# The experts' width in two chunks of 1408 instead of 1024, 1024 and 768, smaller weight units in byte rings, and the sixteen experts written out

## The chip, the core and the metric

The kernel runs on one core of one Trainium2 chip. The metric is the device time in microseconds of one execution, given as the median of three runs. The names of the engines are those of the profile: PE is TensorE (matmuls and transposes), PEld its weight loads, DVE is VectorE, ACT is ScalarE, POOL is GpSimd and SP is SyncE, which here only issues DMAs.

## The reference

The reference is one layer of a hybrid diffusion block: a mixer (long convolutions and a state-space model) and then a mixture of 16 experts, in which each expert picks 128 of the 1024 latent tokens. Only the mixture is touched by the change:

```python
def expert_choice_ffn(h, router_w, w_gate, w_up, w_down):
    n, dm = h.shape[1], h.shape[2]
    cap = CAPACITY_FACTOR * n // N_EXPERTS
    aff = jax.nn.softmax(jnp.einsum('bnd,de->bne', h, router_w).astype(jnp.float32), axis=-1)
    gates, idx = lax.top_k(jnp.swapaxes(aff, 1, 2), cap)
    xg = jax.vmap(lambda hb, ib: hb[ib])(h, idx)
    def expert(args):
        xe, wg, wu, wd = args
        return (jax.nn.silu(xe @ wg) * (xe @ wu)) @ wd
    ...
```

For each expert xe is 128 x 1024, gate and up weights are 1024 x 2816, the down weight is 2816 x 1024, all in float32. That is 34.6 MB of weights for each expert and 554 MB for the sixteen; every weight is read once.

## The kernel before

The program has six stages: prepare, mix, long_convs, output_and_route, experts and finish. The stage experts takes most of the span, and the change lies in it, in the class Weights that lays out its weights, and in two numbers of output_and_route.

**Three products for one.** PE multiplies in the type fp32r, and to keep float32's precision each operand is split in a high part (ACT copies it to fp32r, L2117) and a low part (DVE subtracts the high part from the original, L2152, in place over the original). PE then multiplies high by high, low by high and high by low (L2085 to L2087 for gate and up, L2098 for down). So each weight passes from HBM by a DMA (L1963) to ACT, to DVE and to PE.

**Units.** The weights of an expert come in 18 units, which all engines count in the same order. The width of 2816 is cut into chunks of 1024, 1024 and 768. Each chunk has four units: gate and up, each in two halves of four contraction tiles (4 x 1024 or 4 x 768 elements in each partition). Units 12 to 17 are the down weights, five of four tiles and one of two. A unit has one of six slots of 16 KB for the original and the low part, and one of three slots of 16 KB for the high part.

**The order on each engine** is written out by hand and kept by semaphores. While PE multiplies unit n, ACT makes the high part of unit n + 2 and DVE the low part of unit n + 1. A high part may be written once PE has done with the unit three before it (`used`), and SP may issue a load once PE has done with the unit six before it. Between these stand the other steps of an expert:

- after the gate half of a chunk, ACT takes Silu from PSUM (L2134); after the up half DVE multiplies it by up (L2170); one unit later PE transposes the product (L2066), ACT and DVE make its high and low part (L2138, L2174). PE waits for this low part (`alo`) at the first down unit that uses it.
- the tokens of the next expert are gathered by POOL (L2037), transposed by PE after unit 15 (L2055), and split by ACT (L2121, `high_tokens`) and DVE (L2156, `low_tokens`) in the step of unit 16.
- at the end of an expert DVE scales the result in PSUM to SBUF (L2179) and POOL adds it to the output in HBM (L2043).

DVE's last steps for an expert e stand in this order:

```python
    elif not last_e:
        low_part(e + 1, 0)
...
dve.wait_ge(used, multiplied(e, UNITS - 1))
dve.wait_ge(idxr, 2 * e + 1)
nc.vector.scalar_tensor_tensor(ye, ps[:, 6:8, :]..., ALU.mult, ALU.mult).then_inc(yev, 1)
```

The first fifteen experts are one hardware loop on each engine (`experts_of`, Fori, L1998), the sixteenth is written out behind it.

Of the kernel before, what the change touches and what calls it, by code (L numbers as in the profile page):

```python
# [7 lines left out]
F32 = mybir.dt.float32  # L8
# [1675 lines left out]
def output_and_route(k):  # L1684
# [26 lines left out]
    with nc.Block() as block:  # L1711
        @block.sync
        def _(sp):
# [10 lines left out]
            for n in range(3):  # L1724
                k.weights.load(sp, 0, n)
# [3 lines left out]
            for n in range(3, k.weights.NS):  # L1729
                k.weights.load(sp, 0, n)  # L1730
# [198 lines left out]
class Weights:  # L1929
# [3 lines left out]
    chunks = [(0, 1024), (1024, 1024), (2048, FF - 2048)]  # L1933
    NCW = len(chunks)
    FT = FF // P
    KH = KD // 2
    NS, NHI = 6, 3
    DOWN = 4 * NCW
    tiles = [min(4, FF // P - 4 * d) for d in range(-(-FF // 512))]
    UNITS = DOWN + len(tiles)  # L1940

    def __init__(self, k):
        assert self.UNITS % self.NS == 0 and self.UNITS % self.NHI == 0
        self.raw = [k.over(f"w_raw{s}", 16 * s, 16, F32) for s in range(self.NS)]
        self.got = [k.ctx.enter_context(k.nc.semaphore(f"e_got{s}")) for s in range(self.NS)]
        self.gate_up = [k.i[n].rearrange("l e (k p) f -> l e p k f", p=P) for n in ("ex_w_gate", "ex_w_up")]
        self.down = [k.i["ex_w_down"][:, :, 512 * d:512 * d + P * t, :].rearrange("l e (p f) n -> l e p f n", p=P) for d, t in enumerate(self.tiles)]

    def elements(self, n):
        return self.KH * self.chunks[n // 4][1] if n < self.DOWN else self.tiles[n - self.DOWN] * D  # L1950

    def load(self, eng, e, n):
        s, w = n % self.NS, self.elements(n)
        if n < self.DOWN:
            f0, cols = self.chunks[n // 4]
            k0 = self.KH * (n % 2)
            src = self.gate_up[n % 4 // 2][0, bass.ds(e, 1), :, k0:k0 + self.KH, f0:f0 + cols].rearrange("e p k f -> p (e k) f")
            dst = self.raw[s][:, 0:w].rearrange("p (k f) -> p k f", k=self.KH)
        else:
            d = n - self.DOWN  # L1960
            src = self.down[d][0, bass.ds(e, 1)].rearrange("e p f n -> p (e f) n")
            dst = self.raw[s][:, 0:w].rearrange("p (f n) -> p f n", f=self.tiles[d])
        eng.dma_start(dst, src).then_inc(self.got[s], 16)  # L1963


def experts(k):
# [9 lines left out]
    chunks, KH, NCW, FT, NS, NHI, UNITS, DOWN, tiles = wt.chunks, wt.KH, wt.NCW, wt.FT, wt.NS, wt.NHI, wt.UNITS, wt.DOWN, wt.tiles  # L1976
    raw, got, elements = wt.raw, wt.got, wt.elements
    XT_AT = DOWN + 3
    low = [k.over(f"w_low{s}", 16 * s, 16) for s in range(NS)]
# [290 lines left out]
```

## Time and profile before

| | |
|---|---|
| time, median of 3 runs | 2529.84 us (2527.51 to 2533.13) |
| span of the profiled execution, first to last instruction | 2529.5 us |
| PE busy | 2333.7 us (92%) |
| DVE busy | 1938.6 us (77%) |
| ACT busy | 1315.8 us (52%) |
| the experts, PE's first matmul to its last | 964.1 us to 2492.1 us |
| DMA rate between 1200 and 1400 us | 374 GB/s |

The profiled execution's span differs by 0.3 us from the median of the runs; the profile gives no other time for that execution, so spans can be read as times here. Busy times are averages over six stages with different limits. PE's matmuls are pipelined: the duration that a row gives for one is longer than the distance from its start to the next one's start, and it is this distance that sets how long a row of them takes.

### The profile page before, as it was taken

How to read it: one execution, taken by the hardware profiler on the slowest of the kernel's cores; microseconds unless marked ns; L12 is line 12 of the kernel's file. 1: busy time of each engine (PE TensorE's matmuls, PEld its weight loads, DVE VectorE, ACT ScalarE, POOL GpSimd, SP SyncE). 2: the span in 40 equal slices, each digit the busy share in tenths (PEclk: the TensorE clock that was granted, in tenths of full speed). 3: DMA queues.
4: the chain of work that ended last, by engine and by line, in shares of the span. 5: the costliest groups of instructions: out<-in, count | busy, mean ns of one | idle time of the engine just before them, and what ended most of it. 6: DMA issues, size and time to landing. Idle time of an engine off the chain costs nothing. (4 is left out here: it accounts for less than half of the span.)

```text
span 2529.5 us, 28055 instructions
## 1 busy us (share of the span) xinstructions
PE 2333.7 (92%) x10978; PEld 1775.4 (70%) x10978; DVE 1938.6 (77%) x1434; ACT 1315.8 (52%) x789; POOL 351.5 (14%) x187
## 2 busy tenths in 40 slices
PE   7887889999989937999999999999999999999994
PEld 2323777853445836888888888888888888888883
DVE  5765799837574467888888888888888888888884
ACT  2123422210023116777777777777777777677673
POOL 0533400000002000102102102112112012012010
PEclk9888999999999968999999999999999999999997
DMA  7656344554432155999999999999999999999994
GB/s 272 224 213 248 128 121 126 137 211 150 147 145 93 76 233 209 382 370 368 382 374 362 380 375 367 380 372 371 378 372 371 378 374 368 378 377 366 377 368 158
DMA packets 199200, 725.86 MB, mean 287 GB/s; under 512 B 14035, under 2 KB 60019, under 8 KB 180134
## 3 DMA queue, kind: packets, MB, share of 16 engines
q1 hardware_dynamic: 190878, 694.03, 72.9%
q0 software_dynamic: 5184, 20.97, 3.1%
q10 hardware_dynamic: 3080, 10.09, 1.1%
q8 instruction: 37, 0.61, 0.1%
q14 instruction: 21, 0.16, 0.0%
HBM read 677.87 MB, written 47.17 MB: 287 GB/s over the span
## 5 line engine op out<-in xcount | busy, mean ns | idle before, releaser
L2152 DVE TENSOR_TENSOR w_low<-w_raw,w_high 128x4096 fp32r<-128x4096 f32 (+2 forms) x288 | 1164.0, 4065 | 94.0 <-ACT w_high L2117 94.0
L2117 ACT ACTIVATE w_high<-w_raw 128x4096 fp32r<-128x4096 f32 (+2 forms) x288 | 964.2, 3349 | 470.5 <-PE psum L2087 260.5
L2085 PE MATMUL psum<-w_high,x_high 128*128 128x512 f32 (+1 forms) x1536 | 578.0, 376 | 20.0 <-DVE w_low L2152 17.5
L2086 PE MATMUL psum<-w_low,x_high 128*128 128x512 f32 (+1 forms) x1536 | 573.4, 373 | 0.0
L2087 PE MATMUL psum<-w_high,x_low 128*128 128x512 f32 (+1 forms) x1536 | 572.0, 372 | 0.0
L2085 PEld LDWEIGHTS psum<-w_high,x_high 128*128 128x128 f32 x1536 | 290.0, 189 | 80.7 <-DVE w_low L2152 25.0
L2087 PEld LDWEIGHTS psum<-w_high,x_low 128*128 128x128 f32 x1536 | 289.1, 188 | 52.3
L2086 PEld LDWEIGHTS psum<-w_low,x_high 128*128 128x128 f32 x1536 | 289.7, 189 | 49.8
L2098 PE MATMUL psum<-w_high,a_high 128*128 128x512 f32 x704 | 220.7, 395 | 0.0
L2098 PE MATMUL psum<-w_low,a_high 128*128 128x512 f32 x704 | 217.3, 390 | 0.0
L2098 PE MATMUL psum<-w_high,a_low 128*128 128x512 f32 x704 | 217.0, 389 | 0.0
L2042 POOL TENSOR_TENSOR arena<-arena 1x1 f32<-1x1 f32 x15 | 63.3, 4219 | 1089.0 <-DVE arena L2179 1089.0
L2098 PEld LDWEIGHTS psum<-w_high,a_low 128*128 128x128 f32 x704 | 132.1, 188 | 28.1
L2098 PEld LDWEIGHTS psum<-w_low,a_high 128*128 128x128 f32 x704 | 132.1, 188 | 27.9
L2098 PEld LDWEIGHTS psum<-w_high,a_high 128*128 128x128 f32 x704 | 128.8, 188 | 24.0
L1510 PE MATMUL psum<-arena 128*128 128x512 f32 x256 | 113.2, 605 | 1.7 <-PEq L173 1.7
L2174 DVE TENSOR_TENSOR a_low<-psum,a_high 128x1024 fp32r<-128x1024 f32 (+1 forms) x48 | 54.5, 1136 | 62.4 <-ACT a_high L2138 62.4
L1087 PE MATMUL psum<-p_xhigh,p_whigh 128*128 128x512 f32 x256 | 101.9, 398 | 0.0
L1089 PE MATMUL psum<-p_xhigh,p_wlow 128*128 128x512 f32 x256 | 99.8, 390 | 0.0
L1088 PE MATMUL psum<-p_xlow,p_whigh 128*128 128x512 f32 x256 | 99.8, 390 | 0.0
L2043 POOL DMA_INDIRECT scratch_moe<-arena x16 | 85.4, 5336 | 77.8 <-DVE arena L2179 75.4
L1510 PEld LDWEIGHTS psum<-arena 128*128 128x128 f32 x256 | 49.6, 194 | 64.5 <-issue 64.5
(351 smaller groups left out, 2626.5 us busy)
## 6 DMA issues: line engine op xcount, KB each, us to landing
w_raw<-in_ex_w_down SPq DMA_DIRECT2D x80, 2048.0 KB, 9.5
w_raw<-in_ex_w_gate SPq DMA_DIRECT2D x64, 2048.0 KB, 9.8
w_raw<-in_ex_w_up SPq DMA_DIRECT2D x64, 2048.0 KB, 9.9
w_raw<-in_ex_w_gate SPq DMA_DIRECT2D x32, 1536.0 KB, 10.3
w_raw<-in_ex_w_up SPq DMA_DIRECT2D x32, 1536.0 KB, 7.6
arena<-in_mod_w SPq DMA_DIRECT2D x24, 1024.0 KB, 6.5
w_raw<-in_ex_w_down SPq DMA_DIRECT2D x16, 1024.0 KB, 8.3
scratch_spec<-arena SPq DMA_DIRECT2D x8, 1024.0 KB, 10.7
```

The source lines that it names most:

```text
L1087: nc.tensor.matmul(o, whigh[n % NW][:, kk], high[:, kk, t], start=kk == 0, stop=False)
L1088: nc.tensor.matmul(o, whigh[n % NW][:, kk], low[:, kk, t], start=False, stop=False)
L1089: last = nc.tensor.matmul(o, wlow[n % NW][:, kk], high[:, kk, t], start=False, stop=kk == KD - 1)
L1510: last = nc.tensor.matmul(ps[:, bank(order, f) + mat, :], m[:, mat, kk, :], k.v[:, 4 * (mat % 2) + kk, :], start=kk == 0, stop=kk == 3)
L2042: nc.gpsimd.tensor_tensor(spare, spare, spare, ALU.add).then_inc(spared, 1)
L2043: pool.indirect_dma_start(k.moe, bass.IndirectOffsetOnAxis(ap=k.idx_now, axis=0), ye, None, compute_op=ALU.add).then_inc(put, 16)
L2085: nc.tensor.matmul(o, xt_h[:, x], h[:, f], start=kk == 0, stop=False)
L2086: nc.tensor.matmul(o, xt_h[:, x], l[:, f], start=False, stop=False)
L2087: last = nc.tensor.matmul(o, xt_l[:, x], h[:, f], start=False, stop=kk == KD - 1)
L2098: last = nc.tensor.matmul(ps[:, 6 + half, :], x[:, a], m[:, i * D + half * 512:i * D + (half + 1) * 512], start=f == 0 and first, stop=f = ...
L2117: nc.scalar.activation(high[n % NHI][:, 0:w], raw[n % NS][:, 0:w], ACT.Copy).then_inc(hi_done, 1)
L2152: nc.vector.tensor_tensor(low[n % NS][:, 0:w], raw[n % NS][:, 0:w], high[n % NHI][:, 0:w].bitcast(F32), ALU.subtract).then_inc(lo_done, 1)
```

## The change

The width of 2816 is cut into two chunks of 1408. A gate or up unit has two contraction tiles (2 x 1408 = 2816 elements in each partition), so an expert has 16 gate and up units and 8 down units of 3, 3, 3, 2, 3, 3, 3 and 2 tiles: 24 units in place of 18. Each row of gate or up is loaded in pieces of 1408 elements (5632 bytes) in place of 1024 or 768. The units lie one behind another in a ring of 88 KB (originals and low parts, before 96 KB) and a ring of 44 KB (high parts, before 48 KB); how far back the unit lies whose place a unit takes is worked out by `back`: it gives 8 units for gate and up and 7 or 8 for down in the first ring, and 4 in the second, 3 for the down units 16 to 18. A chunk now fills three PSUM banks, so a row of matmuls has 512, 512 and 384 columns. The products of a chunk are transposed after units 9 and 16 (`ACT_AT`), the tokens after unit 19 (`XT_AT`). Four units instead of three are loaded ahead of the last waits of output_and_route, and eight instead of six before the experts start. The loop over fifteen experts is replaced by sixteen written out on every engine.

```diff
-    chunks = [(0, 1024), (1024, 1024), (2048, FF - 2048)]
+    cols = FF // 2
+    chunks = [(0, cols), (cols, cols)]
     NCW = len(chunks)
...
-    KH = KD // 2
-    NS, NHI = 6, 3
-    DOWN = 4 * NCW
-    tiles = [min(4, FF // P - 4 * d) for d in range(-(-FF // 512))]
+    KH = 2
+    PARTS = KD // KH
+    DOWN = 2 * NCW * PARTS
+    tiles = [3, 3, 3, 2] * NCW
+    first = [sum(([3, 3, 3, 2] * 2)[:d]) for d in range(8)]
     UNITS = DOWN + len(tiles)
+    SLOTS = 8
+    RAW, HIGH = 88, 44
...
-        assert self.UNITS % self.NS == 0 and self.UNITS % self.NHI == 0
-        self.raw = [k.over(f"w_raw{s}", 16 * s, 16, F32) for s in range(self.NS)]
-        self.got = [k.ctx.enter_context(k.nc.semaphore(f"e_got{s}")) for s in range(self.NS)]
+        size = [self.KH * self.cols // 256] * self.DOWN + [4 * t for t in self.tiles]
+        at = [sum(size[:n]) for n in range(self.UNITS)]
+        assert sum(size) % self.RAW == 0 and sum(size) % self.HIGH == 0
+        self.raw_back, self.high_back = (self.back(at, size, ring) for ring in (self.RAW, self.HIGH))
+        self.lead = max(self.raw_back + self.high_back)
+        made = {}
+
+        def over(name, first, n, dtype):
+            key = (name, first, n)
+            if key not in made:
+                made[key] = k.over(f"w_{name}{first}_{n}", first, n, dtype)
+            return made[key]
+
+        self.raw = [over("raw", a % self.RAW, n, F32) for a, n in zip(at, size)]
+        self.low = [over("low", a % self.RAW, n, F32R) for a, n in zip(at, size)]
+        self.high = [over("high", self.RAW + a % self.HIGH, n, F32R) for a, n in zip(at, size)]
+        self.got = [k.ctx.enter_context(k.nc.semaphore(f"e_got{s}")) for s in range(self.SLOTS + len(self.tiles))]
...
+    def back(self, at, size, ring):
+
+        total, out = sum(size), []
+        for n in range(self.UNITS):
+            a, b = at[n] + total - ring, at[n] + size[n] + total - ring
+            units = [m for m in range(2 * self.UNITS) if at[m % self.UNITS] + total * (m // self.UNITS) < b
+                     and at[m % self.UNITS] + size[m % self.UNITS] + total * (m // self.UNITS) > a]
+            out.append(n + self.UNITS - max(units))
+        return out
+
+    def slot(self, n):
+        return n % self.SLOTS if n < self.DOWN else self.SLOTS + n - self.DOWN
+
+    def landed(self, e, n):
+
+        if n < self.DOWN:
+            return e * (16 * self.DOWN // self.SLOTS) + 16 * (n // self.SLOTS + 1)
+        return e * 16 + 16
...
+    ACT_AT, XT_AT = (2 * PARTS + 1, DOWN), DOWN + 3
+    act_bank = (3, 0)
...
+    span = lambda b: ps[:, b:b + 3, :].rearrange("p b n -> p (b n)")[:, 0:w]
+    tokens_in = ps[:, 3:5, :].rearrange("p b n -> p (b n)")
+    at_cols = lambda c: slice(c * w, c * w + w)
...
     def experts_of(eng, body):
-        with eng.Fori(0, NE - 1) as e:
-            body(e, False)
-        body(NE - 1, True)
+        for e in range(NE):
+            body(e, e == NE - 1)
     def multiplied(e, n):
-        return e * UNITS + n + 1 + NS
+        return e * UNITS + n + 1 + wt.lead
...
-                    sp.wait_ge(used, multiplied(e, n - NS))
+                    sp.wait_ge(used, multiplied(e, n - wt.raw_back[n]))
                     wt.load(sp, e, n)
-            loads(0, NS)
-            with sp.Fori(1, NE) as e:
+            loads(0, wt.SLOTS)
+            for e in range(1, NE):
                 loads(e, 0)
...
-                        c, up, w = n // 4, n % 4 // 2, chunks[n // 4][1]
-                        if c and n % 2 == 0:
-                            pe.wait_ge(amul if up else silu, e * NCW + c)
+                        c, up, part = n // (2 * PARTS), n // PARTS % 2, n % PARTS
+                        if c and part == 0:
+                            pe.wait_ge(alo if up else silu, e * NCW + c)
...
-                            for b in range(2):
+                            for b in range(3):
                                 n0, n1 = 512 * b, min(512 * (b + 1), w)
                                 f = slice(kl * w + n0, kl * w + n1)
-                                o = ps[:, 2 * up + b, 0:n1 - n0]
+                                o = ps[:, 3 * up + b, 0:n1 - n0]
...
-                        pe.wait_ge(alo, e * NCW + d // 2 + 1)
+                        pe.wait_ge(alo, e * NCW + d // (len(tiles) // NCW) + 1)
                         if d == 0:
                             pe.wait_ge(yev, e + 1)
...
-                    if n and n % 4 == 0 and n <= DOWN:
-                        transpose_act(e, n // 4 - 1)
+                    if n in ACT_AT:
+                        transpose_act(e, ACT_AT.index(n))
                     if n == XT_AT and not last_e:
-                        pe.wait_ge(alo, e * NCW + NCW)
                         transpose_tokens(e * 16 + 32)
...
-                    if n % 4 == 2 and n < DOWN:
-                        c, w = n // 4, chunks[n // 4][1]
+                    if n < DOWN and n % (2 * PARTS) == PARTS:
+                        c = n // (2 * PARTS)
                         act.wait_ge(used, multiplied(e, n - 1))
                         if c:
                             act.wait_ge(amul, e * NCW + c)
-                        nc.scalar.activation(sg[:, 0:w], two(0, w), ACT.Silu).then_inc(silu, 1)
-                    if n % 4 == 1 and 5 <= n <= DOWN + 1:
-                        c = n // 4 - 1
+                        nc.scalar.activation(sg, span(0), ACT.Silu).then_inc(silu, 1)
+                    if n - 1 in ACT_AT:
+                        c = ACT_AT.index(n - 1)
                         act.wait_ge(atr, e * NCW + c + 1)
-                        nc.scalar.activation(at_h[:, at_cols(c)], two(4, chunks[c][1]), ACT.Copy).then_inc(ahi, 1)
+                        nc.scalar.activation(at_h[:, at_cols(c)], span(act_bank[c]), ACT.Copy).then_inc(ahi, 1)
                     if n == XT_AT + 1 and not last_e:
                         high_tokens(e + 1)
...
-                    if n and n % 4 == 0 and n <= DOWN:
-                        c, w = n // 4 - 1, chunks[n // 4 - 1][1]
+                    if n and n % (2 * PARTS) == 0 and n <= DOWN:
+                        c = n // (2 * PARTS) - 1
                         dve.wait_ge(silu, e * NCW + c + 1)
                         dve.wait_ge(used, multiplied(e, n - 1))
                         if c:
                             dve.wait_ge(atr, e * NCW + c)
-                        nc.vector.tensor_tensor(act_[:, 0:w], sg[:, 0:w], two(2, w), ALU.mult).then_inc(amul, 1)
...
+                        nc.vector.tensor_tensor(act_, sg, span(3), ALU.mult).then_inc(amul, 1)
+                    if n - 1 in ACT_AT:
+                        c = ACT_AT.index(n - 1)
                         dve.wait_ge(ahi, e * NCW + c + 1)
-                        nc.vector.tensor_tensor(at_l[:, at_cols(c)], two(4, chunks[c][1]), at_f[:, at_cols(c)], ALU.subtract).then_inc(alo, 1)
+                        nc.vector.tensor_tensor(at_l[:, at_cols(c)], span(act_bank[c]), at_f[:, at_cols(c)], ALU.subtract).then_inc(alo, 1)
                     if n == XT_AT + 1 and not last_e:
                         low_tokens(e + 1)
```

On DVE this is what stands around the edge between two experts. Before, at the end of the loop's body (units 17 of this expert, the tokens and unit 0 of the next, the result) and the head of the body (the low part of unit 1):

```order
L2152 TENSOR_TENSOR w_low_6540<-w_raw_78,w_high_6543 128x2048
L2156 TENSOR_TENSOR x_low<-psum,x_high 128x1024
L2152 TENSOR_TENSOR w_low_6535<-w_raw_73,w_high_6541 128x4096
L2179 SCALAR_TENSOR_TENSOR arena<-psum,arena 128x1024
L2152 TENSOR_TENSOR w_low_6536<-w_raw_74,w_high_6542 128x4096
```

Of the change, at the same place (units 21, tokens, 22, 23, then units 0, the result, and units 1 and 2 of the next expert):

```order
L2181 TENSOR_TENSOR w_low_12_102<-w_raw_12_86,w_high_12_110 128x3072
L2185 TENSOR_TENSOR x_low<-psum,x_high 128x1024
L2181 TENSOR_TENSOR w_low_12_103<-w_raw_12_87,w_high_12_111 128x3072
L2181 TENSOR_TENSOR w_low_8_104<-w_raw_8_88,w_high_8_112 128x2048
L2181 TENSOR_TENSOR w_low_11_89<-w_raw_11_73,w_high_11_105 128x2816
L2208 SCALAR_TENSOR_TENSOR arena<-psum,arena 128x1024
L2181 TENSOR_TENSOR w_low_11_90<-w_raw_11_74,w_high_11_106 128x2816
L2181 TENSOR_TENSOR w_low_11_91<-w_raw_11_75,w_high_11_107 128x2816
```

The tokens' low part has moved from directly ahead of unit 0's low part to three weight units ahead of it. The result still stands between the low parts of units 0 and 1.

On DVE at the end of the second chunk (low parts of the down units 16 and 17, the product of Silu and up, unit 18, the low part of the transposed product, unit 19), of the change:

```order
L2181 TENSOR_TENSOR w_low_12_97<-w_raw_12_81,w_high_12_109 128x3072
L2181 TENSOR_TENSOR w_low_12_98<-w_raw_12_82,w_high_12_110 128x3072
L2199 TENSOR_TENSOR arena<-arena,psum 128x1408
L2181 TENSOR_TENSOR w_low_12_99<-w_raw_12_83,w_high_12_111 128x3072
L2203 TENSOR_TENSOR a_low<-psum,a_high 128x1408
L2181 TENSOR_TENSOR w_low_8_100<-w_raw_8_84,w_high_8_112 128x2048
```

Before, the last chunk's product had the same place among units of another size (units 12 and 13, the product of 768, unit 14):

```order
L2152 TENSOR_TENSOR w_low_6535<-w_raw_73,w_high_6541 128x4096
L2152 TENSOR_TENSOR w_low_6536<-w_raw_74,w_high_6542 128x4096
L2170 TENSOR_TENSOR arena<-arena,psum 128x768
L2152 TENSOR_TENSOR w_low_6537<-w_raw_75,w_high_6543 128x4096
```

The product stands behind the low part of the unit after the one that PE multiplies, before and now; its width has gone from 768 to 1408.

## Rows read from the trace of the kernel before

**Rows 1.** The page's busy times.

```profile
PE 2333.7 (92%) x10978; PEld 1775.4 (70%) x10978; DVE 1938.6 (77%) x1434; ACT 1315.8 (52%) x789; POOL 351.5 (14%) x187
```

**Rows 2.** Windows: length, busy (x count) by engine, PEclk, DMA share, GB/s.

```profile
922.00:930.00 8.00, 0.00 (x0) 0.00 (x0) 7.72 (x19) 0.00 (x0) 0.00 (x0) 0.50 1.03 410
1147.30:1242.80 95.50, 94.34 (x451) 78.91 (x450) 81.11 (x26) 68.70 (x27) 15.45 (x6) 1.00 0.97 373
```

**Rows 3.** Waits from 1062 to 2399 us: total, times, longest.

```profile
ACT w_high L2117 <- PE psum L2087: 222.1, 140, 2.7
...
PE psum L2085 <- DVE w_low L2152: 16.3, 14, 1.2
```

**Rows 4.** Timeline of PE: start, length, instruction, count [idle before <-releaser].

```profile
1157.73 0.50 PE L2085 MATMUL psum<-w_high,x_high 128*128 128x512 f32 x1 [1.16 <-DVE w_low L2152]
...
1251.40 0.61 PE L2098 MATMUL psum<-w_high,a_low 128*128 128x512 f32 x2
...
1537.89 0.61 PE L2098 MATMUL psum<-w_high,a_low 128*128 128x512 f32 x2
1539.66 0.50 PE L2085 MATMUL psum<-w_high,x_high 128*128 128x512 f32 x1 [1.16 <-DVE w_low L2152]
1540.00 0.40 PE L2086 MATMUL psum<-w_low,x_high 128*128 128x512 f32 x1
...
1541.39 0.39 PE L2086 MATMUL psum<-w_low,x_high 128*128 128x512 f32 x1
...
1545.03 0.39 PE L2087 MATMUL psum<-w_high,x_low 128*128 128x512 f32 x1
...
2399.08 0.47 PE L2085 MATMUL psum<-w_high,x_high 128*128 128x512 f32 x1 [1.26 <-DVE w_low L2152]
...
2491.89 0.61 PE L2098 MATMUL psum<-w_high,a_low 128*128 128x512 f32 x2
```

**Rows 5.** Timeline of DVE around an edge, and at the end.

```profile
1534.05 1.23 DVE L2156 TENSOR_TENSOR x_low<-psum,x_high 128x1024 fp32r<-128x1024 f32 x1 [5.16 <-ACT x_high L2121]
1535.19 4.42 DVE L2152 TENSOR_TENSOR w_low<-w_raw,w_high 128x4096 fp32r<-128x4096 f32 x1
1539.53 1.28 DVE L2179 SCALAR_TENSOR_TENSOR arena<-psum,arena 128x1024 f32<-128x1024 f32 x1
1540.72 8.75 DVE L2152 TENSOR_TENSOR w_low<-w_raw,w_high 128x4096 fp32r<-128x4096 f32 x2
...
2492.54 1.28 DVE L2179 SCALAR_TENSOR_TENSOR arena<-psum,arena 128x1024 f32<-128x1024 f32 x1 [8.68 <-PE psum L2098]
```

**Rows 6.** Timeline of PE: 512 and 256 columns, and the steps after transposes.

```profile
1503.53 0.40 PE L2085 MATMUL psum<-w_high,x_high 128*128 128x512 f32 x1
...
1504.22 0.28 PE L2085 MATMUL psum<-w_high,x_high 128*128 128x256 f32 x1
...
1504.58 0.40 PE L2085 MATMUL psum<-w_high,x_high 128*128 128x512 f32 x1
...
1529.28 1.03 PE L2055 MATMUL psum<-arena 128*128 128x128 f32 x8
1530.07 0.71 PE L2098 MATMUL psum<-w_high,a_high 128*128 128x512 f32 x2
```

**Rows 7.** Groups by shape, 1062 to 2399 us: busy, mean ns of one.

```profile
L2152 DVE TENSOR_TENSOR w_low<-w_raw,w_high 128x3072 fp32r<-128x3072 f32 x56 | 187.8, 3354 | 31.2 <-ACT w_high L2117 31.2
L2117 ACT ACTIVATE w_high<-w_raw 128x3072 fp32r<-128x3072 f32 x56 | 155.5, 2777 | 107.9 <-PE psum L2087 107.9
L2170 DVE TENSOR_TENSOR arena<-arena,psum 128x1024 f32<-128x1024 f32 x28 | 34.0, 1214 | 0.0
L2170 DVE TENSOR_TENSOR arena<-arena,psum 128x768 f32<-128x768 f32 x14 | 13.3, 948 | 0.0
```

**Rows 8.** The page's instruction queue, and the unit loads' time from issue to landing.

```profile
q8 instruction: 37, 0.61, 0.1%
...
DMA to landing us min/median/max: 6.4/9.6/23.9
```

More of the change, by code:

```diff
@@ L1723, in _ @@
                 sp.dma_start(k.h2[m * P:(m + 1) * P, :], h2[:, m % 2, :]).then_inc(put[m % 2], 16)
-            for n in range(3):
+            for n in range(4):
                 k.weights.load(sp, 0, n)
@@ L1728, in _ @@
             sp.wait_ge(tr, 8)
-            for n in range(3, k.weights.NS):
+            for n in range(4, k.weights.SLOTS):
                 k.weights.load(sp, 0, n)
@@ new lines, in __init__ @@
+        self.gate_up = [k.i[n].rearrange("l e (k p) f -> l e p k f", p=P) for n in ("ex_w_gate", "ex_w_up")]
+        self.down = [k.i["ex_w_down"][:, :, P * f:P * (f + t), :].rearrange("l e (p f) n -> l e p f n", p=P) for f, t in zip(self.first, self.tiles)]
+    def back(self, at, size, ring):
[6 more added lines that the diff above has]
+        return out
@@ L1975, in experts @@
     wt = k.weights
[L1976 to L1979, printed above, removed]
-    high = [k.over(f"w_high{s}", 16 * (NS + s), 16) for s in range(NHI)]
-    xe = k.at(144, 4)
-    xt_h, xt_l = k.over("x_high", 148, 4), k.over("x_low", 152, 4)
-    at_h, at_l = k.over("a_high", 156, 11), k.over("a_low", 167, 11)
+    KH, NCW, FT, PARTS, UNITS, DOWN, tiles, first = wt.KH, wt.NCW, wt.FT, wt.PARTS, wt.UNITS, wt.DOWN, wt.tiles, wt.first
+    raw, low, high, got, w = wt.raw, wt.low, wt.high, wt.got, wt.cols
+    ACT_AT, XT_AT = (2 * PARTS + 1, DOWN), DOWN + 3
+    act_bank = (3, 0)
+    xe = k.at(132, 4)
+    xt_h, xt_l = k.over("x_high", 136, 4), k.over("x_low", 140, 4)
+    at_h, at_l = k.over("a_high", 144, 11), k.over("a_low", 155, 11)
     xt_f, at_f = xt_h.bitcast(F32), at_h.bitcast(F32)
-    act_, sg = k.at(178, 4), k.at(182, 4)
-    two = lambda b, w: ps[:, b:b + 2, :].rearrange("p b n -> p (b n)")[:, 0:w]
-    at_cols = lambda c: slice(chunks[c][0], chunks[c][0] + chunks[c][1])
+    act_, sg = k.at(166, 5.5), k.at(171.5, 5.5)
+    span = lambda b: ps[:, b:b + 3, :].rearrange("p b n -> p (b n)")[:, 0:w]
+    tokens_in = ps[:, 3:5, :].rearrange("p b n -> p (b n)")
+    at_cols = lambda c: slice(c * w, c * w + w)
     ye = k.extra
@@ L2059, in transpose_act @@
                 pe.wait_ge(amul, e * NCW + c + 1)
[L2060 to L2064 removed]
+                n = len(tiles) // NCW
+                for d in range(c * n, c * n + n):
+                    f, t = first[d] - first[c * n], tiles[d]
+                    cols = act_[:, P * f:P * (f + t)].rearrange("p (j i) -> p i j", i=t)
                     for i in range(t):
[L2066 removed]
+                        b, o = divmod(f + i, 4)
+                        last = nc.tensor.transpose(ps[:, act_bank[c] + b, o * P:(o + 1) * P], cols[:, i, :], k.ident)
                 last.then_inc(atr, 1)
```

52 lines of the change are left out of this document (19 added, 33 removed).

## The prediction

> **What bounds the kernel now.** I read the page's busy times first, then windows by stage, then the waits of the experts' stage, and last the timelines of PE and DVE. PE is busy for 92% of the span [rows 1], and in one whole expert for 94.34 of 95.50 us, at a granted clock of 1.00, which is its upper level of 2.4 GHz; but the same window shows the DMA engines at a share of 0.97 and 373 GB/s [rows 2]. Both look like the bound, and the reader must tell which one is. Two rows do it. When nothing held the loads back, ahead of the first expert, they ran at 410 GB/s [rows 2], 10% above what the experts draw. And in the waits nobody in the weights' chain waits for a load: ACT, the first to touch them, waits for PE to free a high part (222.1 us in 140 waits) [rows 3]. So the loads are paced by PE, and PE is the bound: a microsecond counts if PE stands or multiplies longer.
>
> PE stands once in an expert. One pass from edge to edge takes (2399.08 - 1157.73) / 13 = 95.49 us [rows 4]. At an edge its last pair of matmuls starts at 1537.89; at 0.2275 us for each (16 starts in 1545.03 - 1541.39 = 3.64 us) the next could start at 1538.345, and it starts at 1539.66: 1.32 us lost [rows 4]. The releaser named is the low part of unit 0 [rows 3, 4]. The first matmul after a pause also takes 0.34 us to the next start instead of 0.23, so 0.11 more [rows 4]. The edge costs 1.43 us.
>
> Why is unit 0 late? DVE sat idle for 5.16 us for the tokens' high part, took 1.14 us to the next start for the tokens, and only then made unit 0's low part, 1535.19 to 1539.61 [rows 5]. The tokens stand ahead of it in DVE's order and come late, since PE transposes them after unit 15 of 18.
>
> **The change, term by term**, for one pass.
>
> *Matmuls: 0.* Gate and up have 288 matmuls before (240 of 512 columns, 48 of 256) and 288 after (192 of 512, 96 of 384), with 135,168 columns in both. No row shows 384 columns. Three of 512 take 1504.22 - 1503.53 = 0.69 us, three of 256 0.36 us [rows 6], so 0.23 and 0.12 each. The middle, 0.173 to 0.175, makes the sum equal; the line through two widths is the nearest reading, and I take it. The bounds are the two neighbours: if 384 cost what 256 does, a pass is 96 x 0.053 = 5.1 us shorter, if it cost what 512 does, as much longer. A gate or up unit then takes PE 12 x 0.2275 + 6 x 0.173 = 3.77 us, a down unit of three tiles 18 x 0.2275 = 4.10 us.
>
> *The tokens: -1.43.* After the change they are transposed after unit 19 of 24; behind them come 11 down tiles, 11 x 6 x 0.2275 = 15.0 us, and on DVE two low parts and unit 0's: 3.35 + 2.28 (a third less) + 3.09 = 8.7 us. Unit 0's low part ends some 4 us before PE wants it. The old wait goes.
>
> *The result: +0.86.* What is late next? DVE's order is still: low part of unit 0, result, low part of unit 1. The result can't start before PE's last matmul ends: at the very end PE's last pair starts at 2491.89, would be followed at 2492.345, and the result starts at 2492.54, 0.20 later [rows 4, 5]. From the result's start to the next one's start are 1540.72 - 1539.53 = 1.19 us [rows 5]. A low part of 3072 takes 3.354 us [rows 7], one of 4096 4.42 [rows 5], so one of 2816 takes 3.09. PE starts 0.05 us after a low part's end (1539.61 to 1539.66) [rows 4, 5]. So unit 1 is ready 0.20 + 1.19 + 3.09 + 0.05 = 4.53 us after PE begins unit 0, and PE is done with unit 0 after 3.77: it stands for 0.76 us, and pays the restart of about 0.10. Before, unit 0 lasted 24 x 0.2275 = 5.46 us and started late, and the same chain of 0.20 + 1.19 + 4.42 was just covered. A smaller unit is the smaller cover: DVE needs 3.09 / 2816, PE 3.77 / 2816 for an element, but the result's 1.19 us are not smaller. The high part is no hindrance, since the ring of four frees its place at the end of unit 21.
>
> *Two chunks for three: -0.09.* PE transposes the same 22 tiles in two groups instead of three. After the tokens' eight transposes (0.79 us) the first matmul pair takes longer by about 0.09 (0.71 where a pair takes 0.61 to 0.62) [rows 4, 6]; one such restart goes. The Silu, product and splitting steps are one less each on ACT and DVE, under PE's cover.
>
> *The product at unit 16: +0.08.* High parts 16 and 17 wait for three units back, the second until PE starts unit 15. Counting from PE's start of unit 16, it is made from -3.57 to -0.79 (2.777 us) [rows 7], its low part until 2.57, and then the product of 1408: by 948 ns for 768 and 1214 for 1024 it takes 1.61 us [rows 7], so it ends near 4.1. PE's unit 16 ends at 4.10 and the transposes want the product: they wait 0 to 0.15 us. Before, unit 12 had 5.46 us of cover there. All later parts of that chain have more than 1 us of room by the same durations.
>
> *Written out instead of a loop: 0.* The sixteenth expert was always written out, so the trace has both forms. From first start to last pair the loop's body takes 1251.40 - 1157.73 = 93.67 us, the last expert 2491.89 - 2399.08 = 92.81 us [rows 4]. The difference of 0.86 is the token transposes, which the last has not: 0.79 + 0.09 [rows 6]. Neither form costs PE anything more. The Trainium skill (Runtime: NRT & Kernel Launch, Instruction fetch mechanics) says that sequential code is fetched in the background and that a taken branch can stall on its target page. By that rule the loop's edge would have a price that now comes back; the trace doesn't bear it out, since PE starts 0.05 us after DVE's low part there.
>
> *Loads: 0.* 24 DMAs instead of 18 carry the same bytes. A gate or up unit is 128 x 2816 x 4 = 1.44 MB and lasts PE 3.77 us: 382 GB/s while it lasts, and over a pass (34.6 MB and 1.05 MB of token rows in 94.9 us) 376 GB/s, under the 410 of rows 2. A load may be issued seven or eight units back: at least 6 x 3.77 = 22.6 us before PE wants the unit, 16 us before ACT must begin, against 9.6 us from issue to landing [rows 8]. The Trainium skill (DMA: Bandwidth & Descriptors, Anatomy of one DMA — SWDGE (gpsimd) path) speaks against smaller loads: a fixed cost of about 2.0 us for each. Were they served one after another, that would be an estimated 24 x 2.0 us on top of the bytes, and no pass could take under 120 us; but by the same rule today's 18 would need 115 us and take 95.5, so the fixed parts overlap here.
>
> **The sum.** -1.43 + 0.86 - 0.09 + 0.08 = -0.58 us for a pass, fifteen edges: -8.7 us. Before the first expert and after the last nothing on PE's path changes. The span is 2529.5 us and the median 2529.84, so they can be used alike: 2529.84 - 8.7 = 2521 us.
>
> **Rivals.**
> - *Both waits gone.* If DVE were quicker than my line says, or PE's 384 columns slower at the start of a unit, unit 1 would not be waited for: -1.43 - 0.09 = -1.52 a pass, 2507 us. Against it: the 0.76 us come from four measured steps. It decides at a low part of 2.3 us for 2816 elements, below what 3.354 for 3072 allows. A part of this case is 384 columns cheaper than the line, which has no row against it below 0.12.
> - *No change that can be told (within 0.2%, 5 us, about what a measurement of this kernel can tell from none).* PE's fixed share of a matmul grows with mixed widths: 512 columns take 0.230 between matmuls of 256 [rows 6] and 0.2275 elsewhere. If 384 columns cost 0.179 instead of 0.173, the 0.58 us are gone (96 x 0.006).
> - *Slower: the loads become the bound.* Rows of 5632 bytes were never loaded before, and their rate has no row. A pass needs 35.65 MB; it decides at 35.65 / 95.49 = 373 GB/s, only 9% below the 410. At 360 a pass takes 99.0 us, 15 x 3.5 more: 2582 us. Against it: the present pieces are 4096 and 3072 bytes, the new ones larger, and no piece is smaller than before.
> - *Slower: instructions.* The page counts 37 fetches in 0.61 MB [rows 8]. The engines' instructions are 24,366 in all [rows 1], of which the loop's 14 repeats are 14 x 960 = 13,440 (451 + 450 + 26 + 27 + 6 in a window of one pass [rows 2]); so 37 fetches went with 10,926, and 14 more copies want about 37 x 13,440 / 10,926 = 45 more, through DMA engines that are full. If each made PE stand for 1.1 us (0.1% of 16 engines' 2529.5 us, over 37), it were +50 us, 2571 us. It decides at 8 such stalls. Against it is the last expert, which fetched its code so and lost nothing.
>
> **How the numbers follow.** The forecast case has 0.60, its own range 2516 to 2525. Both waits gone, or cheap 384 columns: 0.12. No change: 0.15. Loads 0.08, instructions 0.05. Faster by over 0.2% are the first two, 0.72; same 0.15; slower 0.13. The range goes from the second case's 2506 to 2530, which leaves out the slower cases and what of the second lies below.
>
> **What would show it.** The changed profile should show PE's wait for DVE's low part once an expert, 0.7 to 0.8 us long, at unit 1 and not at unit 0; no idle time of several us on DVE for the tokens' high part directly ahead of unit 0; starts of 384-column matmuls 0.17 us apart; passes of 94.9 us; ACT still waiting for PE and not for loads. Passes of 94.0 mean that the wait at unit 1 isn't there. The prediction is wrong if ACT waits for a load, if PE shows idle time without a releaser inside a unit, or if the window's rate falls while PE's busy time does.

## The result, and the profile after

The changed kernel took 2535.99 us (median of 16 runs, 2530.11 to 2539.92), the kernel before on the same chip 2529.47 us (16 runs, 2524.59 to 2538.91). The ratio is 1.0021 (95%: 1.0013 to 1.003): slower by 0.21%, or 5.3 us, where 2521 us were predicted.

The page's busy times and the instruction queue of the changed kernel:

```profile
PE 2348.7 (93%) x10978; PEld 1807.8 (71%) x10978; DVE 1942.6 (77%) x1498; ACT 1296.2 (51%) x824; POOL 325.4 (13%) x187
...
q8 instruction: 87, 1.43, 0.2%
```

PE is busy 15.0 us longer than in [rows 1], with the same number of instructions. The two windows of [rows 2] in the changed kernel's trace:

```profile
922.00:930.00 8.00, 0.00 (x0) 0.00 (x0) 7.73 (x19) 0.00 (x0) 0.00 (x0) 0.50 1.02 417
1147.30:1242.80 95.50, 94.92 (x450) 80.62 (x450) 80.93 (x31) 67.25 (x29) 13.20 (x6) 1.00 0.97 374
```

The DMA engines do what they did, the clock is at its upper level as before, and PE is busy for 94.92 us of 95.50 instead of 94.34. So PE stands less and multiplies longer. Its waits, 1062 to 2399 us:

```profile
ACT w_high L2147 <- PE psum L2119: 220.5, 140, 3.9
...
DVE arena L2208 <- PE psum L2130: 59.2, 14, 4.2
...
PE psum L2117 <- DVE w_low L2181: 8.1, 14, 0.6
PEld psum L2098 <- DVE arena L2199: 4.5, 14, 0.3
```

ACT still waits for PE and for no load. PE's wait for a low part fell from 16.3 to 8.1 us in 14 passes [rows 3]. The timeline shows that it is another wait. PE at an edge, with the next edge behind it:

```profile
1349.12 0.62 PE L2130 MATMUL psum<-w_high,a_low 128*128 128x512 f32 x2
1349.58 0.39 PE L2117 MATMUL psum<-w_high,x_high 128*128 128x512 f32 x1
...
1353.20 0.34 PE L2119 MATMUL psum<-w_high,x_low 128*128 128x384 f32 x1
1354.12 0.50 PE L2117 MATMUL psum<-w_high,x_high 128*128 128x512 f32 x1 [0.58 <-DVE w_low L2181]
...
1445.37 0.39 PE L2117 MATMUL psum<-w_high,x_high 128*128 128x512 f32 x1
```

Unit 0 begins 0.46 us after the last pair's start, with no pause. Unit 1 begins 0.92 us after the last matmul of unit 0, of which 0.18 is that matmul: PE stands for 0.74 us. A pass takes 1445.37 - 1349.58 = 95.79 us, 0.30 more than before. DVE around the same edge:

```profile
1342.47 3.09 DVE L2181 TENSOR_TENSOR w_low<-w_raw,w_high 128x2816 fp32r<-128x2816 f32 x1
...
1349.78 1.28 DVE L2208 SCALAR_TENSOR_TENSOR arena<-psum,arena 128x1024 f32<-128x1024 f32 x1 [4.22 <-PE psum L2130]
1350.98 6.08 DVE L2181 TENSOR_TENSOR w_low<-w_raw,w_high 128x2816 fp32r<-128x2816 f32 x2
```

Unit 0's low part is made long before the edge. DVE waits 4.22 us for PE's last matmul, starts the result 0.20 us after it, and only then makes unit 1's low part. This is the chain that the prediction named.

What it didn't name is seen in a unit in the middle of a chunk. PE in unit 2:

```profile
1358.06 0.40 PE L2117 MATMUL psum<-w_high,x_high 128*128 128x512 f32 x1
1358.30 0.39 PE L2118 MATMUL psum<-w_low,x_high 128*128 128x512 f32 x1
1358.53 0.39 PE L2119 MATMUL psum<-w_high,x_low 128*128 128x512 f32 x1
1358.76 0.40 PE L2117 MATMUL psum<-w_high,x_high 128*128 128x512 f32 x1
...
1359.45 0.34 PE L2117 MATMUL psum<-w_high,x_high 128*128 128x384 f32 x1
...
1359.98 0.40 PE L2117 MATMUL psum<-w_high,x_high 128*128 128x512 f32 x1
...
1361.90 0.40 PE L2117 MATMUL psum<-w_high,x_high 128*128 128x512 f32 x1
```

Eighteen matmuls take 1361.90 - 1358.06 = 3.84 us, where 3.77 were predicted, without any wait. The starts in the trace, in nanoseconds from one to the next, say which matmuls are long. They are taken from the same records as the timeline, before its rounding; the rows of the kernel before are of its pass from 1348.69 us:

```
after,  unit 2:  512: 241 224 231 235 229 232   384: 175 175 178   and again the same
before, unit 2:  512: 227 227 226 227 227 226   ... for all 24
before, unit 1:  512: 270 233 236 224 231 236 228 232 231 227 227 226   then 226 to 227
before, unit 10: 512: 233 236 228   256: 117 118 119   512: 236 233 227   256: 113 120 120
```

I say that PE settles when the distances have become equal. In the kernel before, 512 columns settle at 226.7 ns, and after a pause or a group of transposes it takes five to nine matmuls to get there. Its third chunk, where 512 and 256 alternate, never does. In the changed kernel widths alternate in every gate and up unit, and 512 columns take 232 ns on the mean, 384 take 176.

One pass of each, by what PE starts, in us (from each matmul's start to the next start):

| | before | after | difference |
|---|---|---|---|
| gate and up, without the pause and its restart | 60.62 | 61.42 | +0.80 |
| pause and restart at an edge | 1.43 | 0.85 | -0.58 |
| down | 30.24 | 30.26 | +0.02 |
| transposes | 3.18 | 3.27 | +0.09 |

The sum is +0.33, beside 0.30 from the passes. There are fifteen edges but sixteen experts, and the last one pays for its matmuls without saving at an edge behind it: 15 x 0.30 + (0.30 + 0.58) = 5.4 us, beside 5.3 measured.

In one execution the passes agree within 0.2 us from the second expert on, and the whole time is far less steady: in the fourteen profiled executions PE's first matmul of the experts starts anywhere from 957 to 970 us. So below the pass says more of a small change than the ratio does.

### The profile page after: what moved, and what is told of

It is laid out like the page before. It is cut to its first block and busy times, and to the rows that moved or that the text cites. A ratio compares the mean times of both kernels' runs of the same rounds, so it can differ in the third digit from the quotient of the medians.

```text
span 2534.4 us, 26566 instructions
## 1 busy us (share of the span) xinstructions
PE 2348.7 (93%) x10978; PEld 1807.8 (71%) x10978; DVE 1942.6 (77%) x1498; ACT 1296.2 (51%) x824; POOL 325.4 (13%) x187
## 3 DMA queue, kind: packets, MB, share of 16 engines
q8 instruction: 87, 1.43, 0.2%
## 5 line engine op out<-in xcount | busy, mean ns | idle before, releaser
L2181 DVE TENSOR_TENSOR w_low<-w_raw,w_high 128x2816 fp32r<-128x2816 f32 (+2 forms) x384 | 1166.4, 3086 | 81.9 <-ACT w_high L2147 81.9
L2147 ACT ACTIVATE w_high<-w_raw 128x2816 fp32r<-128x2816 f32 (+2 forms) x384 | 981.1, 2560 | 388.0 <-PE psum L2119 251.8
L2074 POOL TENSOR_TENSOR arena<-arena 1x1 f32<-1x1 f32 x15 | 43.7, 2911 | 1124.4 <-issue 1124.4
L1510 PE MATMUL psum<-arena 128*128 128x512 f32 x256 | 111.8, 599 | 1.7 <-PEq L173 1.7
L447 PE MATMUL psum<-arena 128*128 128x512 f32 x192 | 87.1, 605 | 0.6 <-issue 0.6
```

The source lines that it names most:

```text
L447: last = nc.tensor.matmul(o, m[:, 2 * (s % 3) + b, kk, :], seq[:, 2 * r + kk, :], start=kk == 0 and (b == 0 or s % 3 == 0), stop=kk == 1 a ...
L1510: last = nc.tensor.matmul(ps[:, bank(order, f) + mat, :], m[:, mat, kk, :], k.v[:, 4 * (mat % 2) + kk, :], start=kk == 0, stop=kk == 3)
L2074: nc.gpsimd.tensor_tensor(spare, spare, spare, ALU.add).then_inc(spared, 1)
L2147: nc.scalar.activation(high[n], raw[n], ACT.Copy).then_inc(hi_done, 1)
L2181: nc.vector.tensor_tensor(low[n], raw[n], high[n].bitcast(F32), ALU.subtract).then_inc(lo_done, 1)
```

## Experiments

Passes are means over the second to the fifteenth expert; "unit" is a gate or up unit. Theory W says that what costs is PE's change between widths. Its rivals were theory P, the places of the units in the rings or of the columns in PSUM (three banks, the third one partly filled), and theory C, the written-out code. Each batch of runs had its own runs of the kernel before beside it, and ratios are against these.

| run | what | pass us | ratio |
|---|---|---|---|
| before | the kernel before | 95.49 | 1 |
| after | the change | 95.79 | 1.0021 |
| e_equal | 470, 470, 468 columns | 95.83 | 1.0029 |
| e_border | 6 x 512, 6 x 512, 6 x 384 in a unit | 95.63 | 1.0026 |
| e_result | low part of unit 1 ahead of the result | 94.95 | 0.9982 |
| b_out | before, written out | 95.63 | 1.0015 |
| e_468 | three of 468 | 95.47 | one run, 2530.77 us |
| e_512x3 | three of 512 | 99.35 | one run, 2590.98 us |
| b_tokens | before, tokens one unit earlier | 94.73 | 0.9965 |
| b_384 | before, third chunk 384 + 384 | 95.46 | 0.9993 |
| e_448 | three of 448 | 93.80 | one run, 2495.05 us |
| b_both | b_tokens and b_384 | 94.72 | 0.9939 |
| b_all | b_both, unit 1's low part ahead of the result | 94.36 | 0.9937 |
| e_both | e_result and e_border | 94.80 | 0.9957 |

### e_equal: three nearly equal widths

```diff
-  n0, n1 = 512 * b, min(512 * (b + 1), w)
+  n0, n1 = 470 * b, min(470 * (b + 1), w)
```

> The changed kernel with its three matmuls per tile 470, 470 and 468 columns wide instead of 512, 512 and 384; Silu and the product read three pieces of 470. Theory W (after a change of width PE needs some ten matmuls to come back to its shortest distance between starts, so mixed widths never settle): a gate or up unit falls from 3.84 us to 18 x 0.209 = 3.77, 16 units 1.2 us a pass, passes of 94.6 us instead of 95.79, time about 18 us below the changed kernel (2518 us). Theory P (the cost comes from where the units lie in the rings, or from three PSUM banks): units stay at 3.84 us, time 2536. Theory C (it comes from the code written out): the same, 2536.

Measured: 2536.86 us, ratio 1.0029 (1.0017 to 1.0041), passes of 95.83. PE in the first contraction tile of a unit, and its next tile's first matmul:

```profile
1360.87 0.38 PE L2119 MATMUL psum<-w_high,x_high 128*128 128x470 f32 x1
...
1362.15 0.38 PE L2119 MATMUL psum<-w_high,x_high 128*128 128x468 f32 x1
...
1362.79 0.38 PE L2119 MATMUL psum<-w_high,x_high 128*128 128x470 f32 x1
```

Nine take 1.92 us, the same as nine of 512, 512 and 384, and single distances go from 209 to 217 ns in a pattern of nine, without settling. W had promised some 18 us and gave none. Either W is wrong, or 470 and 468 are themselves widths at which PE doesn't settle.

### e_border: fewer changes of width

```diff
-  for kl in range(KH):
-      for b in range(3):
+  for b in range(3):
+      for kl in range(KH):
```

> The changed kernel with the loop over the three column pieces outside that over the two contraction tiles: twelve matmuls of 512 and then six of 384, so the width changes twice in 18 matmuls instead of four times. Theory W: about half of the 0.07 us of a unit comes back, 0.03 to 0.05 us, 0.5 to 0.8 us a pass, time 2524 to 2529. Theories P and C: 2536, no change.

Measured: 2534.33 us, ratio 1.0026 (1.0014 to 1.0037), passes of 95.63, a unit 3.83 us:

```profile
1368.61 0.39 PE L2117 MATMUL psum<-w_high,x_high 128*128 128x512 f32 x1
...
1370.69 0.39 PE L2117 MATMUL psum<-w_high,x_high 128*128 128x512 f32 x1
...
1371.37 0.33 PE L2117 MATMUL psum<-w_high,x_high 128*128 128x384 f32 x1
...
1372.44 0.39 PE L2117 MATMUL psum<-w_high,x_high 128*128 128x512 f32 x1
```

The first nine of 512 columns take 2.08 us (231 ns each), the last three 0.68 (227). So PE does settle after nine matmuls of 512 columns, and with 12 and 6 of them in a row there is little left to enjoy it. Theory W had promised 0.5 to 0.8 us a pass and the run gave 0.15: half the changes of width isn't half the cost. Twelve matmuls of 512 and six of 384 at their settled distances (226.7 ns, and 173.3 as b_384 shows below) would take 3.76 us. The changed kernel is above that by 0.08 in units 2 to 9 (3.84 us) and by 0.07 in units 11 to 15 (3.83), this run by 0.07. A change costs little more when all nine matmuls behind it have the same width than when the next change cuts them off after six. The whole time doesn't tell the run from the changed kernel.

### e_result: the result moved behind unit 1's low part

```diff
   elif not last_e:
       low_part(e + 1, 0)
+      low_part(e + 1, 1)
```

(and step 0 of all experts but the first leaves `low_part(e, 1)` out)

> The changed kernel with DVE making the low part of the next expert's unit 1 before it takes the result from PSUM, instead of behind it. If PE's stand at unit 1 (0.74 us and the slower restart of 0.11) comes from that order, it goes: 0.85 us a pass, passes of 94.9 us, time about 2523. Rival: the stand moves to unit 2 or PE's slow matmuls leave DVE enough time anyway, then under 3 us come back.

Measured: 2525.33 us, ratio 0.9982 (0.9972 to 0.9993), passes of 94.95, 0.84 less. PE at the start of unit 1, and, in a second view, DVE's result:

```profile
1353.97 0.34 PE L2119 MATMUL psum<-w_high,x_low 128*128 128x384 f32 x1
1354.15 0.40 PE L2117 MATMUL psum<-w_high,x_high 128*128 128x512 f32 x1
```

```profile
1350.55 1.28 DVE L2210 SCALAR_TENSOR_TENSOR arena<-psum,arena 128x1024 f32<-128x1024 f32 x1 [1.05 <-PE psum L2130]
```

No pause is left at unit 1, as expected. The term of +0.86 was the place of the result, and it is more than the whole loss: with this one step moved, the ratio to the kernel before lies on the other side of 1.

### b_out: the kernel before, written out

```diff
-  with eng.Fori(0, NE - 1) as e:
-      body(e, False)
-  body(NE - 1, True)
+  for e in range(NE):
+      body(e, e == NE - 1)
```

> The kernel before with its loop over fifteen experts written out on every engine and nothing else. Theory W: 0, passes of 95.5 us, 2529.5 us. Theory C (instruction fetches through full DMA engines slow PE or start later): slower by 3 to 12 us. The page should show some 87 fetches instead of 37.

Measured: 2530.93 us, ratio 1.0015 (1.0003 to 1.0028), passes of 95.63, with 87 fetches in the instruction queue, as many as the changed kernel has. PE at an edge, DVE's low part of unit 0 ahead of it, and the page's line on the queue:

```profile
1345.10 0.61 PE L2097 MATMUL psum<-w_high,a_low 128*128 128x512 f32 x2
1347.03 0.47 PE L2084 MATMUL psum<-w_high,x_high 128*128 128x512 f32 x1 [1.32 <-DVE w_low L2151]
```

```profile
1342.47 4.42 DVE L2151 TENSOR_TENSOR w_low<-w_raw,w_high 128x4096 fp32r<-128x4096 f32 x1
```

```profile
q8 instruction: 87, 1.43, 0.2%
```

From the last pair to unit 0 are 1.93 us here and 1.77 in [rows 4]; over all passes the waiting edge is 0.14 us longer. PE starts 0.14 us after DVE's low part ends (1346.89 to 1347.03) instead of 0.05, which is 0.09 of it; why isn't shown. Fifty more fetches cost PE no stall anywhere else. The ratio is less clear: 1.0015 is 3.8 us, within what theory C allowed, while fifteen passes give 2.1. The Trainium skill (Runtime: NRT & Kernel Launch, Instruction fetch mechanics) lets one expect the opposite at the edge, since there a taken branch can stall and sequential code is fetched ahead; this trace doesn't agree, by 0.14 us. Nor does b_tokens below, which keeps the loop: its PE starts unit 0 no more than 0.18 us late, and 0.06 us after the low part. The changed kernel doesn't pay the 0.14, since its PE starts unit 0 without waiting and unit 1 0.05 us after its low part.

### e_512x3: three equal widths in three banks

```diff
-  n0, n1 = 512 * b, min(512 * (b + 1), w)
+  n0 = min(512 * b, w - 512); n1 = n0 + 512
```

> The changed kernel with its third matmul 512 columns wide too (columns 896 to 1407, so 128 columns are multiplied twice and the product is taken from wrong places; the output is not the reference's). Rings, units, three banks and the code written out stay. Theory W: the distance settles at 227 ns in every unit. Theory P (placement in the rings or the third bank): 232 ns as in the changed kernel. The pass is longer either way, since 96 matmuls are 128 columns wider: about 5 us a pass at 227 ns.

Measured: 2590.98 us, passes of 99.35. PE, first matmuls of two units:

```profile
1374.02 0.39 PE L2118 MATMUL psum<-w_high,x_high 128*128 128x512 f32 x1
...
1378.10 0.39 PE L2118 MATMUL psum<-w_high,x_high 128*128 128x512 f32 x1
```

18 take 4.08 us, 226.7 ns each. The banks in use, the rings, the units and the written-out code are those of the changed kernel, and only the width is uniform: PE settles as in the kernel before. That rules out the rings, the use of a third bank and the written-out code for the 192 matmuls of 512 columns. Whether a bank that 384 columns fill only in part slows those is a question that this run leaves to the next.

### b_384: the kernel before, third chunk in two equal widths

```diff
-  n0, n1 = 512 * b, min(512 * (b + 1), w)
+  q = 384 if w == 768 else 512
+  n0, n1 = q * b, q * (b + 1)
```

(and Silu and the product read two pieces of 384 in the third chunk)

> The kernel before with the third chunk's 768 columns multiplied as 384 and 384 instead of 512 and 256. Theory W: within units 8 to 11 no width changes, so after a transition they settle at 384 / 2.4 + 13.3 = 173.3 ns, 4.16 us a unit instead of 4.20, 0.1 to 0.17 us a pass, 2 to 3 us in all. Rival X (widths other than 512 never reach the short distance): 176 ns, 4.22 us a unit, no gain. The distances in the trace decide, not the time.

Measured: 2527.94 us, ratio 0.9993 (0.9983 to 1.0002), passes of 95.46. PE in unit 10, in the third chunk:

```profile
1400.47 0.33 PE L2088 MATMUL psum<-w_high,x_high 128*128 128x384 f32 x1
...
1404.63 0.33 PE L2088 MATMUL psum<-w_high,x_high 128*128 128x384 f32 x1
```

24 of 384 columns take 4.16 us, 173.3 ns each, and the same 9216 columns as 12 of 512 and 12 of 256 take 4.20 in the kernel before. So the line's 0.173 us for 384 columns was right, for a row of them. As part of a row of mixed widths it isn't. Partly filled banks don't keep PE from settling. The ratio can't be told from 1; the units' times can. The pass is only 0.03 us shorter where 0.1 to 0.17 were expected: units 8 and 9 aren't faster than before, as they begin behind a change of width and behind transposes (six slow matmuls of 384, 171 to 185 ns), and at the first down unit PE now comes earlier and loses 0.08 us more than before in waiting for DVE's low part.

### e_468 and e_448: exactly equal widths

```diff
-  n0, n1 = 512 * b, min(512 * (b + 1), w)
+  n0, n1 = q * b, q * (b + 1)        # q = 468, and q = 448
```

(and Silu and the product read three pieces of 470, as in e_equal)

> The changed kernel with three matmuls of exactly 468 columns (four of the 1408 columns are left out of the products, so the output is not the reference's). 470, 470, 468 took 213.4 ns from start to start where 470 / 2.4 + 13.3 = 209 was expected. Theory W (any change of width, even by 2 columns, starts the disturbance anew): here no width changes, so after some ten matmuls of a pass the distance settles at 468 / 2.4 + 13.3 = 208.3 ns. Rival X (only widths of 512, or only the old placement of the units, reach the short distance): about 213 ns all along.

> The changed kernel with three matmuls of exactly 448 columns (64 of the 1408 columns are left out of the products, so the output is not the reference's). 468 columns stayed at a mean of 212 ns and never settled, 384 and 512 did. Theory A (a second condition: the rows that a matmul reads must begin at and be a multiple of 64 bytes; 448 x 4 bytes is, 468 x 4 is not): settles at 448 / 2.4 + 13.3 = 200.0 ns. Rival X (only 512, 384 and 256, the powers and halves, settle): a mean of 204 ns with a pattern of nine.

Measured: with 468 columns passes of 95.47 and distances of 207 to 216 ns, 212 on the mean, never settled; 512 and 384 settle at their columns at 2.4 GHz plus 13.3 ns, which would be 208.3. With 448 columns, passes of 93.80 and two patterns; PE in the units of the first pattern:

```profile
1348.30 0.37 PE L2119 MATMUL psum<-w_high,x_high 128*128 128x448 f32 x1
...
1352.02 0.37 PE L2119 MATMUL psum<-w_high,x_high 128*128 128x448 f32 x1
```

18 take 3.72 us, 206.7 ns each, in units 2 to 9; behind the transposes, in units 11 to 15, distances of 199 to 207 ns repeat, 203 on the mean. The same sum gives 200. The idea that widths which are a multiple of 64 bytes settle at that sum falls with this run: 448 columns are one, settle in eight units, and settle 6.7 ns too high. So uniform widths aren't enough: 468 columns stay 4 ns above the sum all along, which is why e_equal gave nothing, and 448 have two distances in the same pass, so that the width alone doesn't set it. What does stays open.

### b_tokens, b_both, b_all, e_both: the parts put together

```diff
-    XT_AT = DOWN + 3
+    XT_AT = DOWN + 2
```

> The kernel before with the next expert's tokens transposed one unit earlier (after unit 14 instead of 15, so DVE has their low part done before it turns to unit 0). By my account of the edge the wait of 1.32 us for unit 0 goes, and the result's place ahead of unit 1's low part then shows as 0.20 + 1.19 + 4.42 + 0.05 - 5.46 = 0.40 us and a restart: -1.43 + 0.5 = -0.9 us a pass, 2515 us. Rival: ACT and DVE have no room a unit earlier and another unit comes late; then under 5 us come back.

> The kernel before with the tokens one unit earlier and the third chunk as 384 and 384. The passes of the two parts alone were 94.72 and 95.45 us against 95.49, so 94.68 us and 2517 us, if they add.

> The kernel of b_both with DVE making the low part of unit 1 ahead of the result. Unit 1's high part waits for the ring of three and is ready 3.8 us after PE begins the last unit, so its low part ends 8.3 us after that and PE wants it after 2.73 + 5.46 = 8.2: the stand of 0.33 us at unit 1 becomes about 0.1, and the result's 1.19 us then make unit 2 late by 0.1 to 0.3 us. Passes of 94.4 to 94.7 us, 2513 to 2518 us.

> The changed kernel with the result behind unit 1's low part and the twelve matmuls of 512 ahead of the six of 384. Passes were 94.95 and 95.64 us apart against 95.79, so 94.80 us if they add, and 2523 us. Were the 512-column matmuls' slow distance the whole of what my sum missed, both together would still be 0.5 us a pass above my 94.3 for that kernel.

b_tokens changes one number in the kernel before: 2518.11 us, ratio 0.9965 (0.9951 to 0.9978), passes of 94.73, 0.76 less where 0.9 were expected. Its PE at unit 0 and at unit 1, and then its DVE ahead of unit 0:

```profile
1343.80 0.61 PE L2098 MATMUL psum<-w_high,a_low 128*128 128x512 f32 x2
1344.44 0.50 PE L2085 MATMUL psum<-w_high,x_high 128*128 128x512 f32 x1
...
1349.79 0.39 PE L2087 MATMUL psum<-w_high,x_low 128*128 128x512 f32 x1
1350.34 0.50 PE L2085 MATMUL psum<-w_high,x_high 128*128 128x512 f32 x1 [0.16 <-DVE w_low L2152]
```

```profile
1339.96 4.42 DVE L2152 TENSOR_TENSOR w_low<-w_raw,w_high 128x4096 fp32r<-128x4096 f32 x1 [3.73 <-ACT w_high L2117]
1344.66 1.28 DVE L2179 SCALAR_TENSOR_TENSOR arena<-psum,arena 128x1024 f32<-128x1024 f32 x1 [0.28 <-PE psum L2098]
```

Of the edge's 1.43 us 0.29 are left. Unit 0 starts 0.64 us after the last pair's start instead of 0.46, so it is 0.18 late, and a restart of 0.11 follows; DVE made its low part just too late, since it waited for ACT's high part and no longer for the tokens. And unit 1 is waited for by 0.55 - 0.23 = 0.32 us, plus a restart: the chain behind the result, which was just covered while unit 0 began late, is not covered any more. b_both adds b_384: 2517.91 us, 0.9939 (0.9923 to 0.9955), in passes no different from those of b_tokens (94.72), so the equal third chunk adds nothing that is seen, and the two ratios, which come from different batches, differ by spread. b_all also moves the low part ahead of the result: passes of 94.36, 2516.74 us, 0.9937 (0.9923 to 0.9951); its pause moved on to unit 2, whose first two matmuls start 260 to 294 ns apart instead of 227. e_both, the changed kernel with both of its repairs, has 94.80 and 2522.16 us, 0.9957 (0.9943 to 0.9971). So the best of them is b_all, the kernel before with its tokens and unit 1's low part earlier, 1.13 us a pass or about 0.6% faster (b_tokens alone 0.35%), and the change of chunks and units isn't needed for it.

## Why the prediction was wrong

Right, with what was measured for one pass:

- *The tokens, -1.43.* Gone, as predicted: unit 0 starts 0.46 us after the last pair. b_tokens shows that the place of the tokens gives 1.14 of it without smaller units.
- *The result, +0.86.* 0.74 of standing and 0.11 of restart, 0.85. e_result takes out 0.84. The kernel before's "just covered" was almost so: it stood 0.04 to 0.06 us at unit 1 (the 270 ns above).
- *Two chunks, -0.09.* In both kernels the distance after the first matmul behind a group of transposes is 313 to 316 ns instead of 227, so one group less gives 0.09.
- *The product at unit 16, +0.08.* The mechanism was right and the size half: the transposes follow the last pair after 0.52 us instead of the usual 0.46, and the first of them takes 215 ns instead of 109, 0.17 us in all. The down row of the table shows little of it, since the kernel before stood 0.06 us at its first down unit and the changed one doesn't. DVE's product and PE around it:

```profile
1415.55 1.61 DVE L2199 TENSOR_TENSOR arena<-arena,psum 128x1408 f32<-128x1408 f32 x1
...
1416.70 0.61 PE L2130 MATMUL psum<-w_high,a_low 128*128 128x512 f32 x2
1417.22 0.84 PE L2098 MATMUL psum<-arena 128*128 128x128 f32 x5
```

- *Loads, 0, and written out, 0.* No wait for a load; 87 fetches, where 37 + 45 were estimated, and no stall from them. The prediction's 120 us for 24 loads served one after another doesn't follow from its 115 for 18, which makes it 127; a pass of 95.79 us is far below either.

Wrong was one term, *Matmuls: 0*, and in it the step "the line through two widths is the nearest reading". The line's 0.173 us is what 384 columns take in a row of their own (b_384), and 0.227 what 512 take in a row of their own (e_512x3). Alternating, they take 0.176 and 0.232: 96 x 0.003 + 192 x 0.005 = some 1.2 us a pass above the settled distances. The kernel before paid a part of that too, in its third chunk and after its pauses, so that the difference is +0.80 by the table, of which -0.09 is the chunk's restart: the term measures +0.89 where 0 stood. With it -0.58 becomes +0.31, and the passes say +0.30. A smaller slip had no weight while the term was 0: terms inside an expert count sixteen times and not fifteen. The three signs of being wrong that the prediction named (ACT waiting for a load, idle time without a releaser inside a unit, a falling rate) all stayed away; the length of the passes alone, 95.79 where 94.9 stood, gave it away.

The rival "no change that can be told" had this mechanism, a fixed share that grows with mixed widths, and had even its sign in [rows 6], 0.230 for 512 columns between matmuls of 256. I put the growth on the 96 matmuls of 384 columns alone and let it decide at 6 ns for each. The larger part fell on the 192 of 512, which I had taken as known. That is how a case I gave 0.15 came to be the start of a slower one. Neither of the two slower rivals, loads and instructions, happened.

What inside PE makes a width settle, and why 448, 468 and 470 columns don't come down to the sum that holds for 384 and 512, isn't settled by these runs. That mixing 512 and 384 costs is shown by e_512x3 and b_384, in which each width alone takes less; e_border adds only 0.15 us. A reason for it isn't shown.

## What to carry to other kernels

When PE is the bound, cut so that matmuls of one width follow each other in long rows, measure that width's own distance (512 and 384 were good ones here, 448 and 468 not), and take the distance between starts from rows in the same mixture as the new code: the distance for 512 columns was 2% too short here, and the 0.89 us that mixed widths cost in all were more than the 0.58 of stall that the change removed. Make a unit smaller only after asking what of fixed length (here the result's 1.19 us) it has to cover, and put such a step behind the next unit's work on the engine that others wait for. And when a change bundles a layout with a move, try the move alone: one number, the unit after which the tokens are transposed, gave 0.76 us a pass, where the bundle lost 0.30.

## What the runs showed of the hardware

- The distance between matmuls of 512 columns is 226.7 ns when settled, 384 take 173.3, both their columns at 2.4 GHz plus 13.3 ns (e_512x3, b_384); 448 take 206.7 or 203 (e_448), 468 take 212 (e_468) and 470 and 468 together 213 (e_equal). The Trainium skill (TensorE: Matmul & The Clock Gate, "Wait — 56ns, not 53.3ns?") gives columns at 2.4 GHz plus about 2.5 ns for back-to-back matmuls; in this stream of fp32r matmuls, each with a weight load of its own, the fixed share is 13.3 ns at best for 384 and 512 columns, and the measurement decides.
- After a pause, a group of transposes or a change of width, five to nine matmuls of 512 columns take 224 to 241 ns before they settle, and six of 384 take 171 to 185 (b_384), at a granted clock of 1.00 all the while (the window above). It isn't the clock.
- The DMA engines moved 410 and 417 GB/s in the 8 us before the first expert and 373 to 374 over a pass, where PE paces them. Pieces of 5632 bytes did as well as those of 4096 and 3072.
